# One projection step of each pair of heads issued behind the last but one row's first transposes, in the attention of a two-layer trunk

## What is computed

```python
q, k, v, z, f_raw = jnp.split(x @ w_in, [FOX_W, 2 * FOX_W, 3 * FOX_W, 4 * FOX_W], axis=-1)
q = rms_norm(q.reshape(B, S, FOX_HEADS, FOX_DH), q_norm_g)
k = rms_norm(k.reshape(B, S, FOX_HEADS, FOX_DH), k_norm_g)
...
logits = jnp.einsum('bhtd,bshd->bhts', qb, kf) + cb[..., None] - c_t[:, :, None, :]
logits = jnp.where(key_pos[None, :] <= q_pos[:, None], logits, -jnp.inf)
probs = jax.nn.softmax(logits, axis=-1)
return jnp.einsum('bhts,bshd->bthd', probs, vf)
```

## Time and profile before

| what | value |
| --- | --- |
| median of 3 runs | 1701.7 us (1700.54 to 1703.46) |
| profiled execution | 1701.29 us |
| its span, first to last instruction | 1699.6 us |
| PE busy | 1658.9 us, 98% of the span |
| ACT busy | 811.2 us, 48% |
| DVE busy | 943.0 us, 55% |
| attention phase | about 1047 to 1499 us of the span |

### The profile page before, as it was taken

The page is one execution under the profiler, slowest core; times in us unless marked ns, Lnnn a source line. Parts: engine busy times, 40 slices in busy tenths (PEclk is TensorE's granted clock), DMA queues, the critical chain, the costliest instruction groups (busy, mean ns, idle before and its releaser), DMA issues. The chain is left out here.

```text
span 1699.6 us, 28841 instructions
## 1 busy us (share of the span) xinstructions
PE 1658.9 (98%) x11160; PEld 1271.1 (75%) x11160; DVE 943.0 (55%) x1730; ACT 811.2 (48%) x1309; POOL 277.1 (16%) x240
## 2 busy tenths in 40 slices
PE   9999999999999989989999999999999999999998
PEld 6777778787777868878888788666666666678787
DVE  5747566675757653874474272354444544559633
ACT  4736455573755562242233342656556655641411
POOL 5213212221312131000000001222212221300000
PEclk9999999999999999999999999999999999999999
DMA  7211010311101031241122023111111111232311
GB/s 163 59 32 38 26 51 13 53 36 39 39 26 39 26 125 41 75 144 46 44 77 74 13 62 76 40 44 33 48 32 44 32 33 41 71 118 78 133 47 53
DMA packets 119943, 96.26 MB, mean 57 GB/s; under 512 B 19904, under 2 KB 103552, under 8 KB 119808
## 3 DMA queue, kind: packets, MB, share of 16 engines
q1 hardware_dynamic: 119808, 94.43, 19.3%
HBM read 85.92 MB, written 8.49 MB: 56 GB/s over the span
## 5 line engine op out<-in xcount | busy, mean ns | idle before, releaser
L466 PE MATMUL gdn_unit<-part_hi,weights_hi 128*128 128x512 f32 x496 | 225.6, 455 | 0.0
L468 PE MATMUL gdn_unit<-part_hi,weights_lo 128*128 128x512 f32 x496 | 195.5, 394 | 0.0
L467 PE MATMUL gdn_unit<-part_lo,weights_hi 128*128 128x512 f32 x496 | 194.3, 392 | 0.0
L2671 DVE CUSTOM_DVE_ANT_0 fa_probs<-fa_scores,fa_decay 128x896 f32<-128x896 f32 (+7 forms) x128 | 97.0, 758 | 118.8 <-PE fa_scores L2458 71.4
L906 DVE SCALAR_TENSOR_TENSOR x<-gdn_raw,gdn_taps,x 128x512 f32<-128x512 f32 x144 | 129.3, 898 | 24.0 <-ACT x L703 19.1
L2608 ACT ACTIVATE fa_probs_t<-fa_turned 128x512 f32<-128x512 f32 (+1 forms) x96 | 52.3, 544 | 140.2 <-PE fa_turned L2475 139.7
L429 POOL TENSOR_TENSOR weights_lo<-ring,weights_hi 128x1024 fp32r<-128x1024 f32 x31 | 75.1, 2424 | 250.3 <-ACT weights_hi L683 250.3
L468 PEld LDWEIGHTS gdn_unit<-part_hi,weights_lo 128*128 128x128 f32 x496 | 93.1, 188 | 20.6
L2587 ACT ACTIVATE fa_probs<-fa_probs,fa_top 128x896 f32<-128x896 f32 (+7 forms) x128 | 99.4, 777 | 18.3 <-DVE fa_top L2671 14.6
L1385 PE MATMUL e_gate<-e_w_hi,part_hi 128*128 128x512 f32 (+1 forms) x272 | 104.7, 385 | 1.9 <-DVE e_w_lo L1605 1.2
L466 PEld LDWEIGHTS gdn_unit<-part_hi,weights_hi 128*128 128x128 f32 x496 | 93.9, 189 | 15.9 <-issue 3.6
(11 more groups left out here) (394 smaller groups left out, 3693.6 us busy)
## 6 DMA issues: line engine op xcount, KB each, us to landing
ring<-in_gdn_w_in_dram SPq DMA_DIRECT2D x31, 512.0 KB, 4.4
ring<-in_fox_w_in_dram SPq DMA_DIRECT2D x20, 512.0 KB, 4.8
fa_decay<-c_rows_scratch SPq DMA_DIRECT2D x64, 128.0 KB, 3.0
e_more_raw<-in_ple_w_gate_dram SPq DMA_DIRECT2D x20, 256.0 KB, 5.2
gdn_g_bc<-g_rows_scratch SPq DMA_DIRECT2D x8, 512.0 KB, 8.5
ring<-in_fox_w_in_dram SPq DMA_DIRECT2D x16, 256.0 KB, 2.8
ring<-in_fox_w_out_dram SPq DMA_DIRECT2D x16, 256.0 KB, 3.4
m_old<-x_scratch SPq DMA_DIRECT2D x8, 512.0 KB, 3.5
```

The lines of the kernel that those rows point to most:

```text
L466: pe.matmul(out, w_hi[:, j % 2, k, :], xh[:, k, ts], start=(k == 0), stop=False)
L467: pe.matmul(out, w_hi[:, j % 2, k, :], xl[:, k, ts], start=False, stop=False)
L468: mm = pe.matmul(out, w_lo[:, j % 2, k, :], xh[:, k, ts], start=False, stop=(k == KT - 1))
L2671: step(dve.tensor_tensor_reduce(probs[:, n % 3, blocks(e)], scores[head][:, blocks(e)], decay[:, head, blocks(e)], 1.0, 3e38, ALU.add, ALU ...
```

## The change

One step of the 32 moves. Behind the scores of row 0 there are three steps instead of four, and the block of `e = 7` gets one, behind the first of its two groups of transposes. The total stays 32. Since the steps are issued in sequence, every step from 11 on takes the place that the next one had. The ACT program changes alike.

```diff
@@ PE
                     if e == 0:
-                        fill(4)
+                        fill(3)
                         continue
...
                             if p >= 0:
                                 turn(p, e - 1, side, by)
-                            if e < NT - 1:
+                            if e < NT - 1 or by == turn_order(e - 1)[0]:
                                 fill(1)
@@ ACT
                     if e == 0:
-                        fill(4)
+                        fill(3)
                         if p >= 0:
                             exponent(p, e, 0)
...
                         if p >= 0:
                             take_turned(p, e - 1, side)
-                        if e < NT - 1:
-                            fill(1)
+                        fill(1)
                         if p >= 0 and side == 0:
                             exponent(p, e, 0)
```

## The result

The changed kernel takes 1720.33 us (median of 4 runs, 1719.44 to 1721.86) against 1702.35 us of the kernel before beside it (1700.54 to 1703.46): 18.0 us or 1.1% slower, ratio 1.0108 with a 95% interval of 1.0097 to 1.0120. The forecast was 1718 in a range of 1710 to 1724, slower.

A forecast was written before the change was run, and what follows sets the result against it. PE was taken to bound the passes; -0.20 + 0.67 + 0.89 + 0.89 = 2.25 us per pass, 15.8 over seven, 16.5 with the last pass, on 1701.29 us profiled, plus 0.4 for the median: 1718 us, range 1710 to 1724.

The forecast's parts named there:

- What bounds: Attention passes: PE, busy 53.0 of 53.8 us, sets the pace, so any PE wait inside a pass adds time seven times.
- The price of the bank: Ends of units: the next unit's first matmul can start 1.14 us behind the last one's issue, after ACT's copy.
- Part 1: Row 0 loses a step: PE gains 0.20 us per pass and idles 0.57 us waiting for DVE.
- Parts 2 and 3: Units 1 and 2 end in rows 2 and 4: PE waits 0.67 and 0.89 us per pass for ACT's copy.
- Rival (c): Row 4: the late weights are not covered, 1.1 us more per pass, 1726 us; chance 0.07.
- Part 4: Row 7 gets step 31: unit 3's copy delays row 7's exponentials, squares and sums, +0.89 us per pass.
- Rival (b): Tail: its delay is absorbed further down, only the bank waits count, 1.36 us per pass, 1712 us; chance 0.10.
- Rival (a): Tail: the step only fills PE's waits and copies don't hold PE up, 1.4 us faster, 1700 us; chance 0.05.
- Part 5: Last pass: row 1's scores gain about 0.1, a product sum ending in row 2's block costs 0.75; together +0.7 us.
- Rival (d): New gaps in the passes: the clock falls to the 1.2 GHz level, 11 us more, 1729 us; chance 0.05.

The follow-up runs named there:

- row0_to_head: Kernel before with one step moved from behind row 0's scores to ahead of them (seven ahead, not six): 1713.07 us, ratio 1.0065.
- row0_to_row1: Kernel before with one step moved from behind row 0's scores to behind the last transposes of row 1's block: 1706.48 us, ratio 1.0026.
- row6_to_row7: Kernel before with only the last of the 32 steps moved, from row 6's block to behind row 7's first transposes: 1708.35 us, ratio 1.0036.
- doubled copies: ACT makes each unit's copy twice in passes 1 to 7: on the kernel before 1702.58 us, ratio 1.0000; on the changed kernel 1734.78 us, ratio 1.0191.
- row0_to_row6: Changed kernel, but its last step stays in row 6's block, ahead of row 7's scores: 1718.03 us, ratio 1.0092 to the kernel before.
- the last two versions: Kernel before with one step ahead of row 0's scores moved up, ahead of the last row's transposes (1700.97 us, ratio 0.9992) or behind them (1701.73, 0.9998).

## Why the prediction was right, point by point

**What bounds.** PE sets the pace in the passes, and the waits inserted at steps 16 and 24 came back in the time of every pass. Right.

**The price of the bank.** Forecast 1.14 us from a last matmul to the first of the next unit, measured 1.24 in rows 2 and 4 (1.23 in row 7) and 1.22 in row0_to_head. The matmul's 0.40, the 0.10 and the copy's 0.60 were as put. The term that was mis-sized is the last one: I took 0.05 us from ACT's end to PE's start from a transpose that waits for an exponential, and for these matmuls it is 0.14 (copy ends at 1145.29, matmul starts at 1145.43). That is 0.08 and 0.06 us in two places, nearly all of what the pass was short: 2.25 forecast, 2.41 measured.

**Part 1.** -0.20 forecast, -0.19 measured, and shown alone by row0_to_row1.

**Parts 2 and 3.** +0.67 and +0.89 forecast, +0.75 and +0.95 measured. The late weights were covered as worked out. DVE's first instruction of row 5 waited 3.88 us for POOL in place of 2.79, and the second came only 0.05 later than PE's own shift puts it (1167.66 for 1162.30 is 5.36 us later, row 5's scores are 5.31 later). Rival (c) fell.

**Part 4.** +0.89 forecast, +0.90 measured, with the chain named: copy, exponentials, squares, sums. Rival (b), that this would be absorbed ahead of row 0's scores, fell: the stretch to the next pair's scores is 0.90 longer, and row6_to_row7 shows it alone. Rival (a) needed the copy to be out within 0.26 to 0.48 us; it took 1.24.

**Part 5.** +0.7 forecast, +1.1 measured up to row 7's scores. This is the weakest term, short in three places. Row 1's scores came 0.90 earlier and ACT's backlog took 0.90 back (the wait of 0.93 at 1478.22), so the gain of 0.1 that I counted was 0. Row 2's stretch cost 0.90 where I had 0.75: the last product's final matmul is issued at 1483.05 and DVE takes the sum from 1483.60, 0.15 us behind its end where I put 0.10, and PE starts at 1484.43, 0.14 behind DVE where I put 0.05. And 0.2 are lost in row 4's block, which I had at nothing. It has one product of 0.68 fewer and is only 0.48 shorter: PE is free at 1498.71, and the transposes start at 1498.92, 0.15 behind the end of an ACT copy of transposes (1498.77). That this copy holds them is read from the times; no run tests it. These misses have the same sign, and the sum stayed in range because they are small.

**The clock.** The windows of 50 us from 1050 to 1500 in the changed kernel's trace all have a granted clock of 1.00, with new idle times of 0.51 to 0.73 us in the passes and 0.93 in the last. (The 0.66 us that the prediction set beside them is of the last pass, rows 7, and not in the windows of rows 1.) Rival (d) fell for the passes. The Trainium skill, "TensorE: Matmul & The Clock Gate", section "A second HAM failure mode: psum-queue depth-cycling", tells of another kernel, in which short idles between groups of matmuls, as it cycles through PSUM banks, let the clock go up and down. With idle times of this size that did not come about here. Even with the doubled copies, whose idle time in row 2 is 1.14 us, the clock shows 1.00 in every one of these windows.

## What to carry to other kernels

When steps of a long accumulation are used as filler and share one PSUM bank, look first at where each accumulation ends. The copy out of the bank needs cover of its own (here 1.24 us from last matmul to first), and shifting steps by one place can uncover several of these ends (here three of four) while the moved step itself costs nothing. In this tail a step that filled PE's wait helped only where it put no new work on ACT, the engine waited for. The last step of a unit does put work on it, a middle one does not. A filler step is worth what it covers at its place, to be read from the distance between the release and the start behind it (here 0.19 of 0.68 us).

## What the runs showed of the hardware beyond that

This is about one drop of the clock that does not go with the change. At the end of the last pass PE has three idle times in a row (0.84, 0.20 and 0.55 us, as before the change, which had 0.84, 0.20 and 0.54), and then issues its warm-up matmuls. In the changed kernel's trace the granted clock is 0.66 in the window from 1515 to 1520 shown above, part of it at the lower level of 1.2 GHz, and 1.00 in the window of the trace before that holds the same place. The twelve warm-ups, the same in both, take 2.56 us there and took 1.50 before (window before, warm-ups after, warm-ups before):

```profile
1495.00:1500.00 5.00, 3.61 (x29) 3.03 (x30) 2.55 (x7) 0.85 (x3) 0.00 (x0) 1.00 0.00 0
```

```profile
1517.20 2.56 PE L125 MATMUL fa_unit<-tri,ident 128*128 128x128 f32 x12
```

```profile
1497.28 1.50 PE L125 MATMUL fa_unit<-tri,ident 128*128 128x128 f32 x12
```

From row 7's last scores to the first matmul behind the warm-ups (L125 into `m_y`) it is 9.88 us (1510.18 to 1520.06), before 8.73 (1490.79 to 1499.52). That is the 1.1 us of the profiled difference. In the other traces these warm-ups take 1.50 us in row6_to_row7 and in the changed kernel with double copies, and 1.95 to 2.77 us in row0_to_row1, row0_to_row6, row0_to_head, the kernel before with double copies and both of the last two versions. So the drop goes neither with the change nor with the length of the idle times ahead of it: the first of them is 0.84 us in kernels with and without the drop, and 1.12 us in both kernels with double copies, of which one has it. Why it comes in some executions was not tested and stays open. Readers of one profiled execution should allow it 1 us here.
